# A hybrid conv and latent-attention step with experts: roots from PSUM, summed squares, embeds without a skew, shared last products

## Chip, core and metric

The kernel runs on one NeuronCore of one Trainium2 chip. The metric is the device time of one execution in microseconds (us). An instruction is named below by its line in the kernel, as L1062. VectorE is DVE in the profile, ScalarE is ACT, TensorE is PE (PEld its weight loads), GpSimd is POOL, SyncE is SP; an engine's name with a q behind it is its DMA queue or sequencer.

## What is computed

Two trunk layers run over 264 tokens (256 of a prompt and 8 samples) of width D = 1024. The mixer of layer 0 is a causal convolution module, that of layer 1 a latent attention with a paged cache.

```python
for i in range(DEPTH):
    hn = rmsnorm(h, norm_mix[i])
    mix = conformer_conv(hn, ...) if i % 2 == 0 else mla_mixer(hn, ...)
    h = h + mix
    h = h + hier_moe(rmsnorm(h, norm_ffn[i]), ...)      # 32 experts in 4 groups, the top 2 of one group
    h = h + (p[i] @ ple_w_in[i]) * jax.nn.sigmoid(rmsnorm(h, ple_g[i]) @ ple_w_gate[i])
return rmsnorm(h, norm_final), conv state, ckv, kpe

def rmsnorm(x, g):
    return x * lax.rsqrt(jnp.mean(x * x, axis=-1, keepdims=True) + EPS) * g
```

The third line of the loop body is called the embed below. The attention normalizes its query and key latents with rmsnorm too, and the convolution module has a layernorm.

## The kernel before

Activations lie transposed: `hT` holds h as 8 chunks (KD = 8) of 128 features by 264 tokens. `xnT` holds the chunks times a gain, `sq` their squares. Weights stream from HBM into nine slots of a ring and a few slots beside it, in an order that SyncE's program fixes; a slot is filled again when TensorE has used it. Each engine has its own program, written out in order, and they meet at semaphores. A result of TensorE goes into one of eight PSUM banks, taken in turn: `arrive` waits until a bank is full, `freed` until its reader has let go of it.

**Norms.** ScalarE squares the chunks, TensorE sums them over features with a product by ones, and the sum lands in a bank. VectorE (`inverse_root`, L1062) takes it times 1/n plus EPS into `rstd`, ScalarE (`root`, L1652) takes the square root in place, VectorE (L1064) the reciprocal. The norms are numbered n0 to n6, `lnv`, `q` and `kv`. The products that need a norm mostly run on values without it, and their results are multiplied by `rstd`.

**Squares that VectorE adds.** For n1, n3, n4 and n6 VectorE adds some of the squares into `sq[:, 0]` (`add_square`, L1086), so that TensorE has fewer to sum.

**Router.** While TensorE makes the output products of the mixer chunk by chunk, it also makes the logits (L534). Then `router_tail` forms each token's sum of squares as a column (`token_sums`, L548): once for the chunks that VectorE added, once for chunk 6, once for chunk 7, three products each. ScalarE copies the logits out (L1658, `lgT` lies in `rstd`), takes the root of the columns (L1660), VectorE sums the three parts and scales before it (L1104 to L1106) and inverts after it (L1108). TensorE turns the logits (L563) and the token rows (L646), and L1188 scales the logits; from there VectorE finds group, experts, ranks and slots, with two products of TensorE between (L656, L662), writes the selection matrix `S` (L1281, L1284), and TensorE gathers the tokens (L682).

**Experts.** 17 pairs of experts are worked off in windows (gate and up L703, down L729, combine L744). SyncE's queue loads their weights (L2036); a load whose slot is in use waits until the products of its pair are done.

**Embed.** TensorE makes eight chunks of the gate product. For each, VectorE multiplies it by `rstd` (L1447), ScalarE takes the sigmoid (L1802), VectorE multiplies by `pinT` (L1450) and adds to h (L1452); in layer 0 it also makes the next mixer's gained chunk (L1456). VectorE's loop is skewed: in round m it does L1447 of chunk m, then the rest of chunk m-1, then the square of chunk m-2 into the sum. ScalarE does sigmoid m, then square m-1 (L1805). TensorE's `last_sum` (L524, L526) closes it with two products: the summed squares, then square 7.

**End.** After n6 VectorE makes eight products of h, gain and `rstd` (L1070), and SyncE stores them in two halves (L2092).

## Time and profile before

| | us |
|---|---|
| median of 3 runs | 910.09 |
| lowest and highest | 907.43 and 912.4 |
| profiled execution | 914.86 |
| its span, first to last instruction | 913.2 |
| TensorE busy | 785.9 |
| VectorE busy | 319.0 |
| ScalarE busy | 206.4 |
| GpSimd busy | 58.9 |

The mean granted TensorE clock of the profiled execution is 0.932 of full. Busy shares say little here, since the stages differ: some are bound by TensorE, the expert stages by the weight stream, and in between there are stretches in which the engines hand over to each other. A row of a timeline gives start, duration, engine, line, operation, what is written and read, how many instructions are merged, and in brackets how long the engine was idle before and what ended that. The releaser is inferred; where the one named had long been done, it was another. fp32 products show as two passes each, so one product is x2.

### The profile page before, as it was taken

What the parts mean: (1) busy time and instruction counts of PE and PEld (TensorE: products, weight loads), DVE (VectorE), ACT (ScalarE), POOL (GpSimd) and SP (SyncE); (2) the same over time, 40 slices, a digit from 0 to 9 for tenths busy, and PEclk for the clock granted to TensorE, in tenths of its full rate; (3) what the DMA queues carried; (4) which work ended last, traced back from release to release, by engine and by line L of the source; (5) the groups of instructions that cost most, each with busy time, mean ns of one, the idle gap of its engine ahead of it and who ended that gap; (6) DMA issues with size and microseconds to landing.
All of it is one profiled execution on the core that took longest, in us unless ns stands there. A gap on an engine that the chain in (4) does not pass through costs nothing.

```text
span 913.2 us, 16409 instructions
## 1 busy us (share of the span) xinstructions
PE 785.9 (86%) x6398; PEld 561.3 (61%) x6398; DVE 319.0 (35%) x948; ACT 206.4 (23%) x492; POOL 58.9 (6%) x101
## 2 busy tenths in 40 slices
PE   5999999799889776889899877999998799697894
PEld 5876667666556554558676554678665466364583
DVE  1433333333313212225346464126133133221435
ACT  2100234321111101022226352015321011110322
POOL 2401000000000000000051700000000000000000
PEclk9999999799999989979999988898999899988898
DMA  9853894389999999983166470896699999999601
GB/s 374 324 170 89 275 402 148 146 334 414 417 415 418 414 417 415 412 337 139 47 216 223 127 281 1 354 417 242 231 394 415 418 414 417 416 416 416 243 1 48
DMA packets 59376, 269.35 MB, mean 295 GB/s; under 512 B 7312, under 2 KB 12384, under 8 KB 38176
## 3 DMA queue, kind: packets, MB, share of 16 engines
q1 hardware_dynamic: 53072, 259.22, 71.7%
q10 hardware_dynamic: 3472, 5.13, 1.8%
q0 software_dynamic: 2752, 3.91, 1.5%
q8 instruction: 53, 0.87, 0.4%
q14 instruction: 27, 0.22, 0.1%
HBM read 261.05 MB, written 2.52 MB: 289 GB/s over the span
## 4 chain that ended last, share of the span: by engine, by line
PE 60%; DMA 27%; SPq 5%; DVE 3%; issue 2%; ACT 2%; ACTq 0%; DVEq 0%
PE bank L572 25%; DMA ring<-in_moe_w_up 19%; PE bank L703 10%; PE bank L682 5%; DMA xn_sq<-in_moe_w_up 5%; SPq L2036 4%; PE bank L744 3%; PE bank L729 3%; PE bank L597 2%; PE bank L971 1%; SPq L2028 1%; PE bank L824 1%; PE bank L534 1%; PE bank L829 1%; PE bank L517 1%
## 5 line engine op out<-in xcount | busy, mean ns | idle before, releaser
L703 PE MATMUL bank<-ring,arena 128*32 128x256 f32 x1344 | 116.4, 406 | 21.9 <-DMA arena<-in_moe_w_up 13.5
L572 PE MATMUL bank<-xn_sq,ring 128*128 128x264 f32 x480 | 110.2, 392 | 9.1 <-DMA ring<-in_stream 9.1
L572 PE MATMUL bank<-arena,ring 128*128 128x264 f32 (+1 forms) x456 | 110.3, 397 | 3.0 <-DVE arena L1482 2.2
L572 PEld LDWEIGHTS bank<-xn_sq,ring 128*128 128x128 f32 x480 | 92.5, 193 | 26.0 <-issue 9.9
L682 PEld LDWEIGHTS bank<-arena 128*128 128x128 f32 x864 | 100.5, 196 | 11.3 <-issue 10.4
L682 PE MATMUL bank<-arena 128*128 128x128 f32 (+1 forms) x864 | 103.7, 281 | 4.3 <-DMA ring<-in_moe_w_down 3.8
L1314 DVE TENSOR_TENSOR arena<-arena,bank 128x128 f32<-128x128 f32 x34 | 9.8, 287 | 267.8 <-ACT arena L1735 267.8
L572 PEld LDWEIGHTS bank<-arena,ring 128*128 128x128 f32 x456 | 87.0, 195 | 24.5 <-issue 8.5
L703 PEld LDWEIGHTS bank<-ring,arena 128*32 128x32 f32 x1344 | 65.0, 117 | 60.1 <-issue 41.2
L744 PE MATMUL bank<-arena 128*128 128x264 f32 (+1 forms) x288 | 73.0, 409 | 5.2 <-ACT arena L1751 5.2
L703 PE MATMUL bank<-xn_sq,arena 128*32 128x256 f32 x384 | 56.9, 463 | 17.2 <-DMA ring<-in_moe_w_up 17.2
L744 PEld LDWEIGHTS bank<-arena 128*128 128x128 f32 (+1 forms) x288 | 55.5, 197 | 24.7 <-ACT arena L1751 9.6
L703 PE MATMUL bank<-arena 128*32 128x256 f32 x448 | 61.3, 436 | 10.6 <-DMA xn_sq<-in_moe_w_up 10.6
L1331 DVE TENSOR_TENSOR hT<-hT,bank 128x264 f32<-128x264 f32 x144 | 61.7, 428 | 23.3 <-PE bank L744 21.2
L729 PE MATMUL bank<-ring,arena 128*32 128x512 f32 x336 | 55.7, 619 | 12.6 <-ACT arena L1742 12.6
L1751 ACT COPY arena<-bank 64x512 f32<-64x512 f32 x68 | 39.4, 580 | 72.5 <-PE bank L729 71.7
L703 PEld LDWEIGHTS bank<-xn_sq,arena 128*32 128x32 f32 x384 | 27.5, 133 | 33.4 <-issue 29.4
L703 PEld LDWEIGHTS bank<-arena 128*32 128x32 f32 x448 | 29.7, 125 | 24.8 <-issue 19.8
L1735 ACT ACTIVATE arena<-bank 128x128 f32<-128x128 f32 x34 | 9.4, 277 | 156.2 <-PE bank L703 156.2
L729 PE MATMUL bank<-arena 128*32 128x512 f32 x208 | 38.4, 598 | 6.4 <-ACT arena L1742 6.4
L1954 POOL DMA_DIRECT2D arena<-in_cache_kpeT x64 | 32.0, 501 | 9.0 <-PE bank L971 4.0
L1647 ACT ACTIVATE xn_sq<-hT 128x264 f32<-128x264 f32 x40 | 16.2, 421 | 71.5 <-DVE hT L1078 64.6
(253 smaller groups left out, 835.1 us busy)
## 6 DMA issues: line engine op xcount, KB each, us to landing
ring<-in_moe_w_gate SPq DMA_DIRECT2D x38, 1024.0 KB, 21.7
ring<-in_moe_w_up SPq DMA_DIRECT2D x38, 1024.0 KB, 21.9
ring<-in_moe_w_down SPq DMA_DIRECT2D x38, 1024.0 KB, 22.8
ring<-in_stream SPq DMA_DIRECT2D x35, 1024.0 KB, 9.3
arena<-in_moe_w_down SPq DMA_DIRECT2D x26, 1024.0 KB, 21.0
arena<-in_moe_w_gate SPq DMA_DIRECT2D x14, 1024.0 KB, 19.7
...
```

What stands on the lines that cost most here:

```text
L572: t = mm(ps[:, 0:cols], lhs(k), rhs(k), start=(k == 0), stop=(k == n - 1))
L597: t = mm(ps[CG * b:CG * (b + 1), 0:TP], dg[:, c, TQ * b + q, :], shifted[p % 2][:, b, c % 2, NQ * q:NQ * q + TP], start=(q == 0), stop=(q ...
L682: t = mm(bank[k // 4][:, (k % 4) * n:(k % 4 + 1) * n], XR[:, i, k * P:(k + 1) * P], S[:, j % 2, i, 0:n], start=(i == 0), stop=(i == 2))
L703: t = mm(bank[2 + r][p0:p0 + U, 0:F].rearrange("p (c f) -> p c f", c=2), x, w[i][:, :, k * F + c * P:k * F + (c + 1) * P], start=(k == 0), ...
L729: t = mm(bank[4 + r][p0:p0 + U, :], hidT[:, r, U * (2 * i + c):U * (2 * i + c + 1)], w[i][:, c, h * 512:(h + 1) * 512], start=(c == 0), st ...
L744: mm(bank[CBANK[k % 4]][:, 0:T], O[0:n, j % 2, k * P:(k + 1) * P], gate[0:n, j % 2, :], start=True, stop=True).then_inc(s_cb, 1)
L1314: v.tensor_tensor(hid[:, q % 2, :], sg[:, q % 2, :], bank[2 + q % 2][:, P:2 * P], ALU.mult)\
L1331: v.tensor_tensor(hT[:, k, :], hT[:, k, :], bank[CBANK[k % 4]][:, 0:T], ALU.add).then_inc(s_add, 1)
L1647: s.activation(sq[:, at + k, :], src[:, k, :], ACT.Square).then_inc(s_sq, 1)
L1751: s.copy(O[64 * r:64 * r + 64, j % 2, 512 * h:512 * (h + 1)], bank[4 + r][64 * h:64 * h + 64, :])\
L1954: pool.dma_start(KPT[DR * i:DR * (i + 1), n * PAGE:(n + 1) * PAGE], a["cache_kpeT"][bass.ds(numbers[i][n], 1)].rearrange("o p f -> p (o f)"))\
L2036: sp.dma_start(d, expert_weights(l, number, c)).then_inc(w_in[PLACE[p]], 16)
```

## The change

Six things change.

- Roots. ScalarE's square root reads the sum from PSUM, with scale 1/n and a bias of EPS (a new column of constants), and writes `rstd`; VectorE's scaling is gone. Before the roots of `q` and `kv` ScalarE waits until the banks before are let go, and for `kv` until the query latents are made.
- Router squares. VectorE adds the squares of chunks 1 to 7 for n1 and n4, so `token_sums` is one group of three products. ScalarE takes the roots of the columns from PSUM in two instructions, and takes a root of one element (`early_root`) before it copies the logits.
- Embed. The skew is gone: a chunk is finished in its own round, and the square of chunk m-1 is added between L1447 and the sigmoid's product of chunk m. ScalarE's order stays.
- Last gain. In layer 1's embed VectorE multiplies each finished chunk by the last gain into `pinT`.
- Last products. They are `pinT` times `rstd`: chunks 0 to 4 on VectorE, 5 to 7 on GpSimd.
- Stores. SyncE stores chunks 0 to 2 and 3 to 4, ScalarE's queue stores 5 to 7, from the arena in place of `xnT`.

```diff
@@ -49,7 +49,7 @@
 ARENA = 22936
...
+C_ID, C_ONE, C_TRI, C_ROT, C_EPS, C_COS, C_SIN = 0, 128, 256, 384, 512, 513, 513 + T
 C_MASK = C_SIN + T
...
@@ -150,8 +150,9 @@
 PIN_LAST = [(), (3, 4, 5, 6, 7)]
 
 
-ADDED = {"n1": (0, KD - 3), "n3": (KD - 3, KD - 2), "n4": (2 * KD - 5, KD - 3), "n6": (3 * KD - 8, KD - 2)}
+ADDED = {"n1": (0, KD - 1), "n3": (KD - 1, KD - 2), "n4": (2 * KD - 3, KD - 1), "n6": (3 * KD - 4, KD - 2)}
 LG = 64
+YV = 5
 NORMS = []
...
@@ -536,27 +540,19 @@
                 if k == KD - 1:
                     t.then_inc(is_full(("router", l)), 1)
 
-            def token_sums(l, x):
-
-                key = "n1" if l == 0 else "n4"
-                if x == 0:
-                    open_bank(pe, ("sums", l))
-                    pe.wait_ge(s_acc, sum(ADDED[key]))
-                else:
-                    pe.wait_ge(s_sq, SQ[key] + KD - 2 + x)
+            def token_sums(l):
+
+                ps = open_bank(pe, ("sums", l))
+                pe.wait_ge(s_acc, sum(ADDED["n1" if l == 0 else "n4"]))
                 for i, (t0, n) in enumerate(TILES):
-                    t = mm(bank[taken["sums", l][0]][0:n, 3 * i + x:3 * i + x + 1],
-                           sq[:, KD - 3 + x if x else 0, t0:t0 + n], ones[:, 0:1], start=True, stop=True)
-                if x == 2:
-                    t.then_inc(is_full(("sums", l)), 1)
+                    t = mm(ps[0:n, i:i + 1], sq[:, 0, t0:t0 + n], ones[:, 0:1], start=True, stop=True)
+                t.then_inc(is_full(("sums", l)), 1)
 
             def router_tail(l, norm):
 
                 logits(l, norm, KD - 2)
-                token_sums(l, 0)
-                token_sums(l, 1)
                 logits(l, norm, KD - 1)
-                token_sums(l, 2)
+                token_sums(l)
                 ps = open_bank(pe, ("lg", l))
                 freed(pe, ("router", l))
                 for i, (t0, n) in enumerate(TILES):
@@ -1056,19 +1052,11 @@
                 ins.then_inc(s_dve, 1)
                 dve.wait_ge(s_dve, steps[0])
 
-            def inverse_root(key, n):
-
-                ps = arrive(dve, key)
-                v.tensor_scalar(rstd[:], ps[:, 0:T], 1.0 / n, EPS, ALU.mult, ALU.add).then_inc(is_free(key), 1)
-                dve.wait_ge(s_rs, NORMS.index(key) + 1)
+            def inverse_root(key):
+
+                freed(dve, key)
                 v.reciprocal(rstd[:], rstd[:]).then_inc(s_inv, 1)
                 dve.wait_ge(s_inv, NORMS.index(key) + 1)
-
-            def norm(key, gain, col):
-                inverse_root(key, D)
-                for k in range(KD):
-                    v.scalar_tensor_tensor(out=xnT[:, k, :], in0=hT[:, k, :], scalar=vcol(gain, col + k), in1=rstd[:],
-                                           op0=ALU.mult, op1=ALU.mult).then_inc(s_xn, 1)
 
             def gained(gain, col, k):
                 v.tensor_scalar(xnT[:, k, :], hT[:, k, :], vcol(gain, col + k), None, ALU.mult).then_inc(s_xn, 1)
@@ -1093,18 +1081,14 @@
                     gained(gain, col, k)
                     if 2 <= k < KD - 1:
                         add_square(key, k - 1)
+                    if k >= KD - 2:
+                        add_square(key, k)
 
             def inverse_columns(l):
 
                 key = ("sums", l)
                 at = NORMS.index("n1" if l == 0 else "n4") + 1
-                ps = arrive(dve, key)
-                x = ps[:, 0:9].rearrange("p (i s) -> p i s", i=3)
-                dve.wait_ge(s_zero, 6)
-                v.reduce_sum(rcol[:, 0:2], x[:, 0:2, :], AX.X)
-                step(v.reduce_sum(rcol[0:TS, 2:3], x[0:TS, 2:3, :], AX.X))
-                v.tensor_scalar(rcol[:], rcol[:], 1.0 / D, EPS, ALU.mult, ALU.add).then_inc(is_free(key), 1)
-                dve.wait_ge(s_rs, at)
+                freed(dve, key)
                 v.reciprocal(rcol[:], rcol[:]).then_inc(s_inv, 1)
                 dve.wait_ge(s_inv, at)
 
...
@@ -1440,30 +1424,29 @@
             def embed(l):
 
                 name = "n3" if l == 0 else "n6"
-                for m in range(KD + 1):
-                    if m < KD:
-                        key = ("pg", l, m)
-                        ps = arrive(dve, key)
-                        v.tensor_tensor(sgp[:, m % 2, :], ps[:, 0:T], rstd[:], ALU.mult).then_inc(is_free(key), 1)
-                    if 1 <= m <= KD:
-                        dve.wait_ge(s_gb, KD * l + m)
-                        step(v.tensor_tensor(tgp[:, (m - 1) % 2, :], sgp[:, (m - 1) % 2, :], pinT[:, m - 1, :],
-                                             ALU.mult))
-                        v.tensor_tensor(hT[:, m - 1, :], hT[:, m - 1, :], tgp[:, (m - 1) % 2, :], ALU.add)\
-                         .then_inc(s_ple, 1)
-                        if l == 0:
-                            dve.wait_ge(s_ple, m)
-                            v.tensor_scalar(xaT[:, m - 1, :], hT[:, m - 1, :], vcol("norm_mix", KD + m - 1), None,
-                                            ALU.mult).then_inc(s_xn, 1)
-                    if 3 <= m <= KD:
-                        add_square(name, m - 2)
+                for m in range(KD):
+                    key = ("pg", l, m)
+                    ps = arrive(dve, key)
+                    v.tensor_tensor(sgp[:, m % 2, :], ps[:, 0:T], rstd[:], ALU.mult).then_inc(is_free(key), 1)
+                    if m >= 2:
+                        add_square(name, m - 1)
+                    dve.wait_ge(s_gb, KD * l + m + 1)
+                    step(v.tensor_tensor(tgp[:, m % 2, :], sgp[:, m % 2, :], pinT[:, m, :], ALU.mult))
+                    v.tensor_tensor(hT[:, m, :], hT[:, m, :], tgp[:, m % 2, :], ALU.add).then_inc(s_ple, 1)
+                    dve.wait_ge(s_ple, KD * l + m + 1)
+                    if l == 0:
+                        v.tensor_scalar(xaT[:, m, :], hT[:, m, :], vcol("norm_mix", KD + m), None, ALU.mult)\
+                         .then_inc(s_xn, 1)
+                    else:
+                        v.tensor_scalar(pinT[:, m, :], hT[:, m, :], vcol("norm_final", m), None, ALU.mult)\
+                         .then_inc(s_fin, 1)
                 dve.wait_ge(s_ple, KD * (l + 1))
 
             dve.wait_ge(s_done, 32)
             moe(0)
-            inverse_root("n2", D)
+            inverse_root("n2")
             embed(0)
-            inverse_root("n3", D)
+            inverse_root("n3")
             for m in range(KQ):
                 ps = arrive(dve, ("cq", m))
                 v.tensor_tensor(cqr[:, m, :], ps[:, 0:T], rstd[:], ALU.mult).then_inc(is_free(("cq", m)), 1)
...
@@ -1628,9 +1611,12 @@
             inverse_columns(1)
             dve.wait_ge(s_done, 32 + 64)
             moe(1)
-            inverse_root("n5", D)
+            inverse_root("n5")
             embed(1)
-            norm("n6", "norm_final", 0)
+            inverse_root("n6")
+            dve.wait_ge(s_fin, KD)
+            for k in range(YV):
+                v.tensor_tensor(pinT[:, k, :], pinT[:, k, :], rstd[:], ALU.mult).then_inc(s_yv, 1)
 
         @block.scalar
         def _(act):
@@ -1646,18 +1632,25 @@
                     ready(k)
                     s.activation(sq[:, at + k, :], src[:, k, :], ACT.Square).then_inc(s_sq, 1)
 
-            def root(key):
-
-                freed(act, key)
-                s.activation(rstd[:], rstd[:], ACT.Sqrt).then_inc(s_rs, 1)
+            eps = cst[:, C_EPS:C_EPS + 1]
+
+            def root(key, n=D):
+
+                ps = arrive(act, key)
+                s.activation(rstd[:], ps[:, 0:T], ACT.Sqrt, bias=eps, scale=1.0 / n).then_inc(is_free(key), 1)
 
             def column_root(l):
 
+                s.activation(early_root[:], ones[0:1, 0:1], ACT.Sqrt)
                 key = ("router", l)
                 ps = arrive(act, key)
                 s.copy(lgT, ps[0:G + E, 0:T]).then_inc(is_free(key), 1)
-                freed(act, ("sums", l))
-                s.activation(rcol[:], rcol[:], ACT.Sqrt).then_inc(s_rs, 1)
+                key = ("sums", l)
+                ps = arrive(act, key)
+                act.wait_ge(s_zero, 6)
+                s.activation(rcol[:, 0:2], ps[:, 0:2], ACT.Sqrt, bias=eps, scale=1.0 / D)
+                s.activation(rcol[0:TS, 2:3], ps[0:TS, 2:3], ACT.Sqrt, bias=eps[0:TS], scale=1.0 / D)\
+                 .then_inc(is_free(key), 1)
 
             def h_ready(key):
                 return lambda k: freed(act, key + (k,))
@@ -1810,8 +1803,11 @@
             root("n3")
             squares("q", cqr, KQ, lambda k: freed(act, ("cq", k)))
             squares("kv", kvr, KK, lambda k: freed(act, ("kv", k)), at=KQ)
-            root("q")
-            root("kv")
+            for key in (*(("cq", m) for m in range(KQ)), *(("kv", m) for m in range(KK)), "kpe"):
+                freed(act, key)
+            root("q", QL)
+            act.wait_ge(s_cq, KQ)
+            root("kv", KL)
             for c in range(4):
                 ps = arrive(act, ("qp", c))
                 s.copy(qpr[:, c, :], ps[:, 0:T]).then_inc(is_free(("qp", c)), 1)
@@ -1887,6 +1883,8 @@
             moe(1)
             embed(1)
             root("n6")
+            act.wait_ge(s_yp, KD - YV)
+            act.dma_start(out["y"][:, YV:KD], pinT[:, YV:KD, :]).then_inc(s_y, 16)
 
         def expert_weights(l, e, c):
 
@@ -1975,6 +1973,10 @@
             arrive(pool, ("ss", 0, 1))
             load_kpe(numbers)
             moe(1)
+            pool.wait_ge(s_fin, KD)
+            pool.wait_ge(s_inv, len(NORMS))
+            for k in range(YV, KD):
+                g.tensor_tensor(pinT[:, k, :], pinT[:, k, :], rstd[:], ALU.mult).then_inc(s_yp, 1)
 
         @block.sync
         def _(sp):
@@ -2087,10 +2089,11 @@
             for g in range(G_PG1, NPIECE):
                 fill(g)
 
-            for k in (0, KD // 2):
-                sp.wait_ge(s_xn, 6 * KD + k + KD // 2)
-                sp.dma_start(out["y"][:, k:k + KD // 2], xnT[:, k:k + KD // 2, :]).then_inc(s_y, 16)
-            sp.wait_ge(s_y, 32)
+            for k in (0, YV - 2):
+                n = YV - 2 if k == 0 else 2
+                sp.wait_ge(s_yv, k + n)
+                sp.dma_start(out["y"][:, k:k + n], pinT[:, k:k + n, :]).then_inc(s_y, 16)
+            sp.wait_ge(s_y, 48)
             sp.wait_ge(s_done, 16 * 6)
```

ScalarE's program in layer 0's router, from the squares (L1647) over the logits copy (L1658) to the token rows (L1710), before:

```order
L1647 ACTIVATE xn_sq<-hT 128x264 x8
L1658 COPY rstd<-bank 36x264
L1660 ACT_TABLE_LOAD
L1660 ACTIVATE rcol<-rcol 128x3
L1710 ACTIVATE arena<-bank,rcol 128x64x8 x4
```

and after:

```order
L1633 ACTIVATE xn_sq<-hT 128x264 x8
L1644 ACT_TABLE_LOAD
L1644 ACTIVATE early_root<-cst 1x1
L1647 COPY rstd<-bank 36x264
L1651 ACTIVATE rcol<-bank,cst 128x2
L1652 ACTIVATE rcol<-bank,cst 8x1
L1703 ACTIVATE arena<-bank,rcol 128x64x8 x4
```

The table load has moved ahead of the logits copy, with the root of one element; the column roots read the bank.

VectorE's program at the end of layer 1's embed, from the gate product of chunk 7 (L1447) to the last products, before:

```order
L1447 TENSOR_TENSOR arena<-bank,rstd 128x264
L1450 TENSOR_TENSOR arena<-arena 128x264
L1452 TENSOR_TENSOR hT<-hT,arena 128x264
L1086 TENSOR_TENSOR xn_sq<-xn_sq 128x264
L1450 TENSOR_TENSOR arena<-arena 128x264
L1452 TENSOR_TENSOR hT<-hT,arena 128x264
L1086 TENSOR_TENSOR xn_sq<-xn_sq 128x264
L1062 TENSOR_SCALAR rstd<-bank 128x264
L1064 RECIPROCAL rstd<-rstd 128x264
L1070 SCALAR_TENSOR_TENSOR xn_sq<-hT,vt,rstd 128x264 x8
```

and after (L1430 is the gate product, L1074 the added square, L1441 the last gain):

```order
L1430 TENSOR_TENSOR arena<-bank,rstd 128x264
L1074 TENSOR_TENSOR xn_sq<-xn_sq 128x264
L1434 TENSOR_TENSOR arena<-arena 128x264
L1435 TENSOR_TENSOR hT<-hT,arena 128x264
L1441 TENSOR_SCALAR arena<-hT,vt 128x264
L1058 RECIPROCAL rstd<-rstd 128x264
L1619 TENSOR_TENSOR arena<-arena,rstd 128x264 x5
```

Behind the gate product of chunk 7 stood seven instructions before the reciprocal, now four, and the added square stands ahead of the chunk's own product.

## Rows read from the trace of the kernel before

**Rows 1.** The page's chain that ended last, shares of the span by engine.
```profile
PE 60%; DMA 27%; SPq 5%; DVE 3%; issue 2%; ACT 2%; ACTq 0%; DVEq 0%
```
**Rows 2.** Timeline, layer 0's router: start, us, engine, line, operation, merged instructions [idle before].
```profile
149.15 0.42 ACT L1647 ACTIVATE xn_sq<-hT 128x264 f32<-128x264 f32 x1 [3.90 <-DVE hT L1078]
...
151.14 0.37 ACT L1658 COPY rstd<-bank 36x264 f32<-36x264 f32 x1 [1.57 <-PE bank L534]
...
153.27 0.57 DVE L1188 SCALAR_TENSOR_TENSOR rt_L<-bank,rcol,br 128x36 f32<-128x36 f32 x3
...
158.38 0.94 PE L656 MATMUL bank<-rt_M,cst 128*128 128x32 f32 x6 [0.45 <-DVE rt_M L1217]
...
164.98 8.24 PE L682 MATMUL bank<-arena 128*128 128x128 f32 x48 [3.76 <-DMA ring<-in_moe_w_down]
...
177.82 0.36 SPq L2036 DMA_DIRECT2D ring<-in_moe_w_gate  x1
```
**Rows 3.** Chain of waits, the row transposes of both layers: start, us, what.
```profile
152.48 2.77 PE bank L646 x24
...
618.72 5.31 PE bank L646 x24
```
**Rows 4.** Windows: stretch, length, busy (x) by engine, PEclk, DMA share, GB/s.
```profile
619.00:622.00 3.00, 3.00 (x16) 3.00 (x15) 2.69 (x19) 2.15 (x3) 0.00 (x0) 0.50 0.97 396
```
**Rows 5.** Timeline, the LayerNorm root.
```profile
111.06 0.43 DVE L1062 TENSOR_SCALAR rstd<-bank 128x264 f32<-128x264 f32 x1 [2.03 <-PE bank L517]
111.53 0.42 ACT L1652 ACTIVATE rstd<-rstd 128x264 f32<-128x264 f32 x1 [0.74 <-DVE rstd L1062]
...
115.04 7.67 PE L572 MATMUL bank<-arena,ring 128*128 128x264 f32 x32 [0.46 <-ACT arena L1687]
```
**Rows 6.** One line, a function with a per-partition bias: min/median/max ns, starts, form.
```profile
L1680 ACT ACTIVATE arena<-arena,vt x8: 514/514/514, 27.9 to 87.0; 128x264 f32<-128x264 f32 x8
```
**Rows 7.** Timeline, the end of layer 0's embed.
```profile
436.75 0.43 DVE L1447 TENSOR_TENSOR arena<-bank,rstd 128x264 f32<-128x264 f32 x1 [1.59 <-PE bank L572]
...
437.22 0.42 ACT L1802 ACTIVATE arena<-arena 128x264 f32<-128x264 f32 x1 [2.33 <-DVE arena L1447]
...
439.84 0.42 DVE L1086 TENSOR_TENSOR xn_sq<-xn_sq 128x264 f32<-128x264 f32 x1
...
440.42 1.22 PE L524 MATMUL bank<-xn_sq,cst 128*128 128x264 f32 x2 [3.70 <-DVE xn_sq L1086]
...
442.31 3.92 PE L572 MATMUL bank<-arena,ring 128*128 128x264 f32 x14
```
**Rows 8.** Windows, the sums of layer 0's embed.
```profile
440.00:442.00 2.00, 1.58 (x4) 1.30 (x5) 0.27 (x1) 1.28 (x1) 0.00 (x0) 0.54 0.38 160
```
**Rows 9.** Timeline, TensorE's first product from the query latents.
```profile
469.35 8.25 PE L572 MATMUL bank<-arena,ring 128*128 128x264 f32 x36 [2.20 <-DVE arena L1482]
```
**Rows 10.** Timeline, the end of the kernel.
```profile
902.66 1.28 ACT L1652 ACT_TABLE_LOAD   x1
...
904.93 1.80 DVE L1064 RECIPROCAL rstd<-rstd 128x264 f32<-128x264 f32 x1 [0.49 <-ACT rstd L1652]
906.77 3.32 DVE L1070 SCALAR_TENSOR_TENSOR xn_sq<-hT,vt,rstd 128x264 f32<-128x264 f32 x8
908.50 1.96 SPq L2092 DMA_DIRECT2D out_y<-xn_sq  x2
```
**Rows 11.** DMA issues of the last 14 us: count, KB each, median us to landing.
```profile
out_y<-xn_sq SPq DMA_DIRECT2D x2, 528.0 KB, 2.7
```
**Rows 12.** Two lines whose instructions meet at 29.4: min/median/max ns, starts, form.
```profile
L1138 DVE SCALAR_TENSOR_TENSOR arena<-arena,vt x8: 222/228/1914, 29.4 to 88.0; 128x8 f32<-128x8 f32 x8
...
L1915 POOL TENSOR_TENSOR arena<-arena,cst x8: 1931/1938/2122, 17.7 to 31.2; 128x1024 f32<-128x1024 f32 x8
```
**Rows 13.** Timeline, ScalarE's first table load and what follows it.
```profile
8.62 1.28 ACT L1647 ACT_TABLE_LOAD   x1 [8.62 <-issue]
9.92 2.61 ACT L1647 ACTIVATE xn_sq<-hT 128x264 f32<-128x264 f32 x8
```

14 lines of the change are left out of this document (8 added, 6 removed).

## Prediction

> **What bounds the kernel now.** I read first the page's chain of waits. TensorE makes 60% of it and transfers 27%, VectorE 3%, ScalarE 2% [rows 1]: only work that TensorE waits for, or that stands at the very end, can pay. Then the timelines of the places that the diff touches, to see who waits for whom there.
>
> In layer 0's router TensorE idles twice: 0.45 us before the counts (L656) and 3.76 us before the first gather (L682), both for VectorE's routing steps [rows 2]. (The row names a transfer; the instruction waits for S, which VectorE had just written.) The expert stream starts again only when the first gate and up products are done, at 177.82 [rows 2], and by the page's slices it then fills the DMA engines at about 415 GB/s. They had drained before, so a router that ends earlier moves the whole stage; nothing downstream eats it.
>
> In layer 1's router TensorE doesn't wait: it is the late one. Its row transposes take 5.31 us against 2.77 in layer 0 [rows 3], at a granted clock of 0.50, that is 1.2 GHz [rows 4].
>
> **LayerNorm root.** Today VectorE scales (111.06, 0.43 us), ScalarE takes the root, VectorE inverts, and TensorE waits 0.46 us for the first silu [rows 5]. The diff drops the scaling with its hand-over, 111.06 to 111.53, 0.47 us. But the new root has eps as a per-partition operand; the nearest row with one takes 514 ns [rows 6] against 0.42 for the root without [rows 5]: 0.09 back. Net 0.38, and TensorE was free to use 0.46. I take **0.36**. The roots n0, n2, n5 gain the same, worth nothing: TensorE streams products past them. Bounds for one root: 0.25 to 0.47.
>
> **Router, layer 0.** The last square ends at 149.57 [rows 2]. VectorE adds it (0.42) by 150.05, and three column products instead of nine follow, so the sums stand before ScalarE can use them. ScalarE meanwhile loads the table (1.28) and does the tiny early root: 149.59 + 1.28 + about 0.2 = 151.07, then the copy of the logits, which today starts at 151.14 [rows 2]. So the logits come out only about 0.1 us earlier, after a pause on TensorE of some 0.7 us that it didn't have. The column roots follow the copy, and the inverse is ready near 152.0. L1188, today 153.27 [rows 2], then waits for the logits alone: about 152.4, 0.9 earlier. TensorE's products up to L656 move only 0.1, so of 158.38 one gets the 0.45 of idle and that 0.1: **0.55**. From there VectorE's steps are as before, up to the gather. Bounds 0.3 to 0.9.
>
> **Router, layer 1.** TensorE is late itself there; only its own 0.1 counts: **0.1**, bounds -0.2 to 0.3.
>
> **Embed, layer 0.** Today's skew leaves chunk 7 to a last round: L1447 at 436.75, the sum of squares at 439.84, TensorE starts the sums at 440.42 and the query products at 442.31 [rows 7]. Now chunk 7 is finished in its own round, but one wait is new. ScalarE's order is unchanged: sigmoid of m, then square of m-1. VectorE now adds square m-1 before it takes sigmoid m, so it stands behind both. Counted out for m = 7: L1447 436.75; sigmoid 437.22 (as today); square 6 after it 437.52 to 437.94; add to 438.40; product 438.33 to 438.75, add to h 438.80 to 439.23, square 7 439.27 to 439.69. TensorE does the first sum at 438.56 and the last at 439.83. The query products start at 440.27 (a pair of passes 0.44) or 440.71 (0.88, half clock). Against 442.31 that is 2.04 or 1.60. Today the granted clock is 0.54 in 440 to 442 [rows 8], after 3.70 us of idle; the query products lose about another 0.6 to it (14 passes in 3.92 us against 3.28 at the later spacing). The new idle before work is about 1.6 and 0.9 us. If the clock holds: 2.04 + 0.6 = 2.64. Two to one that it holds: **2.2**, bounds 1.4 to 2.7. Earlier rounds hide it: a round is 2.9 us of VectorE and ScalarE against 3.56 of TensorE's.
>
> **Query root.** TensorE waits 2.20 us for the scaled latents [rows 9]; the root is in front of them. It waits now for VectorE's last eviction too, which is long past. **0.36**, same bounds. The key root gains as much beside 8 us of query products: nothing. That ScalarE waits there for s_cq delays nothing: it did so through VectorE.
>
> **End, root n6.** Square 7 ends today just before 902.66, where the table load begins that ends at 903.94; the inverse starts at 904.93 [rows 10]. Counted as in the embed, square 7 ends at 902.73, 0.09 later; the load ends at 904.02, the sums are there before, the root takes 0.51, the inverse starts at 904.58: **0.35**. Here the load, no longer the scaling, is what ends last.
>
> **End, products and stores.** Today eight fused products take 3.32 us, the first store goes after four (908.50) [rows 10], each takes 2.7 us [rows 11]. Now five plain ones on VectorE (about 0.36 apart, as the centring ones) and three on GpSimd. The trace holds a GpSimd product, 1.94 us for 1024 columns, so 0.5 for 264; and beside it a VectorE instruction of eight columns took 1914 ns instead of 222 [rows 12]. Both engines' products read two SBUF tensors here too. If they take turns: VectorE's third product at +1.95, GpSimd's third at +2.4, VectorE's fifth at +3.05; the last 264 KB store is issued at +3.15 instead of +3.40, a smaller one, and 1.06 MB must pass from +2.7: landing near +5.4 to +5.5 against +6.1. If they run side by side, the third product ends at +1.1 and all has landed near +4.5. I take turns, **0.6**; bounds -0.5 (GpSimd at 0.9 each) to 1.6. By this the trace agrees with the Trainium skill ("SBUF — State Buffer", Who interferes with whom): a VectorE instruction with two SBUF inputs and a GpSimd one that reads SBUF exclude each other for a whole instruction. Without that rule the term would be 1.6.
>
> **Sum.** 0.36 + 0.55 + 0.1 + 2.2 + 0.36 + 0.35 + 0.6 = 4.5 us. The profiled execution took 914.86 (span 913.2), so 910.3 on its scale. It lies 4.8 above the median of the runs, 910.09; nothing says that what it had extra sits in these terms, so the same 4.5 comes off the median: **905.6**. The three runs spread over 5 us, so I call 0.5%, 4.5 us, what a measurement can tell.
>
> **Rivals.**
> *Fuller gain.* The clock holds in the embed (2.64) and the last products run side by side (1.6): 6.0 off, 904.1. For it: a third of these terms is clock luck. Against: the 1914 ns row. 20%.
> *Swallowed.* The expert stream ends when its bytes have passed, whenever the router ends. Then all before it goes (0.36, 0.55, 2.2, 0.36, 0.1), and 0.95 at the end stays: 909.1. Against: the DMA engines are idle when the stream restarts. 13%.
> *Slower: the clock.* The routers get a pause on TensorE that they didn't have. Layer 1's clock fell in just these steps and cost 2.5 us on the transposes [rows 3, 4]; if layer 0's falls there too, and layer 1's gather runs at half clock like layer 0's (8.2 against 5.6 us), 2.5 + 2.6 plus about 0.8 on the products between is 5.9 against the 4.5: 911.5, slower by 1.4. It decides from 4.5 us of added cost at half clock. Against: the first 160 us ran at full clock with pauses in them. 10%.
> *Load in the way.* If a table load holds ScalarE for longer than its own 1.28, the early root pushes the logits back. With 1.4 more per load: +0.8 and +1.2 in the routers and +1.0 at the end instead of -0.55, -0.1 and -0.35: 909.6. Against: a load at 8.62 of 1.28 us is followed by work at 9.92 [rows 13]. 5%. The Trainium skill ("ScalarE: Activation LUTs", What ACT_TABLE_LOAD costs) adds a drain of 1.38 us to every load; the trace doesn't show it.
> The forecast itself: 52%, with its own range 904.0 to 907.2.
>
> **Numbers.** Range 901.5 to 909.5: the terms' bounds sum to 2 to 7, widened by the clock's shifts and the runs' spread; beyond it lies most of the slower rival. Faster by over 0.5% (below 905.5): half of the forecast, nearly all of the fuller gain, 0.48. Slower by over 0.5%: only the slower rival with a bad draw, 0.05. Same: 0.47.
>
> **What would show it.** The roots read from PSUM at 0.5 us, the inverse 0.36 sooner after the sums. In layer 0's router no idle before the counts product, the logits copy still near 151.1. In the embed square 6 right behind sigmoid 7, VectorE idle about 0.5 us before the add, TensorE back 1.6 to 2 us sooner after its last gate product. At the end VectorE's products spread to 3 us by GpSimd's. Wrong would be: query products that start less than 1.4 us sooner; a stream restart that doesn't move; the five products done in 1.9 us.

## The result and the profile after

The changed kernel takes 903.99 us, median of 22 runs (894.95 to 909.28); the kernel before, beside it, 908.9 (22 runs, 905.45 to 914.14). The ratio is 0.9917 with a 95% interval of 0.9895 to 0.9939: faster by 0.6 to 1.1%. Two of the 22 runs count as slow and the ratio leaves them out; the two medians alone would give 0.9946. Run again later it took 903.54 against 910.12, ratio 0.9929 (0.9907 to 0.9951). The forecast was 905.6, so the gain was underrated (4.5 us against 4.9 and 6.6 between the medians of the two series). That the time still lies so near is luck: as the runs show, terms of the forecast were wrong in opposite directions. The profiled execution took 903.49 (span 901.8, mean granted clock 0.939; before 913.2 and 0.932).

The chain of waits of the changed kernel, shares of the span by engine:

```profile
PE 65%; DMA 20%; SPq 5%; ACT 3%; DVE 3%; issue 2%; DVEq 0%; ACTq 0%
```

TensorE's share is 65% instead of 60 [rows 1], the transfers' 20 instead of 27; it is still these two. The places of the prediction, in the timeline of the changed kernel (columns as in [rows 2]): LayerNorm root, router of layer 0, the turn of layer 0's embed, and the end. Rows in between are left out.

```profile
111.03 0.48 ACT L1640 ACTIVATE rstd<-bank,cst 128x264 f32<-128x264 f32 x1 [0.27 <-PE bank L521]
114.60 2.62 PE L568 MATMUL bank<-arena,ring 128*128 128x264 f32 x10
...
150.57 0.35 ACT L1647 COPY rstd<-bank 36x264 f32<-36x264 f32 x1
151.07 0.76 PE L559 MATMUL bank<-cst,rstd 36*128 36x36 f32 x6 [0.60 <-ACT rstd L1647]
151.97 0.57 DVE L1172 SCALAR_TENSOR_TENSOR rt_L<-bank,rcol,br 128x36 f32<-128x36 f32 x3 [0.53 <-PE bank L559]
157.11 0.91 PE L652 MATMUL bank<-rt_M,cst 128*128 128x32 f32 x6
163.77 1.62 PE L678 MATMUL bank<-arena 128*128 128x128 f32 x6 [4.19 <-DVE arena L1268]
...
430.99 0.43 DVE L1430 TENSOR_TENSOR arena<-bank,rstd 128x264 f32<-128x264 f32 x1 [0.69 <-PE bank L568]
432.23 0.43 DVE L1074 TENSOR_TENSOR xn_sq<-xn_sq 128x264 f32<-128x264 f32 x1 [0.80 <-ACT xn_sq L1798]
432.81 0.69 PE L528 MATMUL bank<-xn_sq,cst 128*128 128x264 f32 x2 [1.85 <-DVE xn_sq L1074]
433.98 1.25 PE L530 MATMUL bank<-xn_sq,cst 128*128 128x264 f32 x2 [0.49 <-ACT xn_sq L1798]
435.02 2.41 PE L568 MATMUL bank<-arena,ring 128*128 128x264 f32 x5
...
888.65 1.28 ACT L1640 ACT_TABLE_LOAD   x1
889.94 0.48 ACT L1640 ACTIVATE rstd<-bank,cst 128x264 f32<-128x264 f32 x1
890.52 1.80 DVE L1058 RECIPROCAL rstd<-rstd 128x264 f32<-128x264 f32 x1 [1.96 <-ACT rstd L1640]
892.36 3.44 DVE L1619 TENSOR_TENSOR arena<-arena,rstd 128x264 f32<-128x264 f32 x5
892.48 2.69 POOL L1979 TENSOR_TENSOR arena<-arena,rstd 128x264 f32<-128x264 f32 x3 [281.56 <-DVE rstd L1058]
894.60 1.57 SPq L2095 DMA_DIRECT2D out_y<-arena  x2
895.21 0.35 ACTq L1887 DMA_DIRECT2D out_y<-arena  x1
```

The root from PSUM takes 0.48, as taken; the silu products start 0.44 sooner than the 115.04 of [rows 5], and 0.43 of it is left where the router begins. The counts product comes 1.27 sooner than the 158.38 of [rows 2], 0.84 of it the router's own. In the embed every wait is the one that was counted: VectorE stands 0.80 for square 6 (the prediction's steps give as much, its last paragraph says 0.5), and from the chunk-7 product to the query products it is 4.03 us where it was 5.56 [rows 7]. The five products take 3.44 us and the three on GpSimd 2.69 beside them: they take turns, at a little more than was counted (VectorE through at +3.5 after the reciprocal instead of +3.05, GpSimd at +2.9 instead of +2.4).

What wasn't foreseen is after the stores. The closing instructions of the engines in the changed kernel (duration in ns, start in us):

```profile
L202 DVEq DRAIN  x1: 3474/3474/3474, 892.4 to 892.4; - x1
L202 POOLq DRAIN  x1: 9035/9035/9035, 892.5 to 892.5; - x1
L202 SPq COMPARE_BRANCH  x1: 41/41/41, 898.8 to 898.8; - x1
```

SyncE is through at 898.8, when the stores have landed: 6.5 us after the reciprocal, where it was 6.1 before (906.7 to 912.8) and 5.45 were predicted. But the kernel ends at 901.8, when GpSimd's closing drain does, 6.35 us after GpSimd's last product. Before, that drain ran long ago:

```profile
L200 POOLq DRAIN  x1: 6357/6357/6357, 636.2 to 636.2; - x1
L200 SPq COMPARE_BRANCH  x1: 41/41/41, 912.8 to 912.8; - x1
```

From the end of the reciprocal to the end of the span it is 9.5 us (892.3 to 901.8) where it was 6.5 (906.7 to 913.2). So 3 us are lost at the end, and yet the kernel gained 5 to 7 between the medians: more was won elsewhere than the prediction had. Two differences stand out, both on TensorE. One lies ahead of layer 1's experts and is taken up at the end, under "Router, layer 1". The other is in the chain of the changed kernel, in layer 0's last gate and up group (64 rows) and what follows:

```profile
380.82 3.61 PE bank L699 x59
384.43 1.89 issue
386.32 0.65 PE bank L699 x5
388.33 1.97 PE bank L725 x16
...
391.56 6.05 PE bank L740 x16
```

and of the kernel before:

```profile
383.15 2.79 PE bank L703 x47
385.94 2.85 issue
388.79 2.15 PE bank L703 x17
392.44 3.62 PE bank L729 x16
```

Before, TensorE stops after 47 rows (its products as the profile counts them, a pass each) for 2.85 us, for nothing that the profile shows (in the program the group waits only ahead of its first product), and then runs at half clock (16 down products in 3.62 us instead of 1.97). Now it stops after 59 rows, for 1.89, and the rest of the group and the down products run at full clock. The clock falls all the same, a few us later, in the combine (L740). The windows show it too (PE, PEld, DVE, ACT, POOL busy, granted clock, DMA share, GB/s), before and then after:

```profile
388.00:396.00 8.00, 6.17 (x34) 1.63 (x33) 0.29 (x1) 0.54 (x2) 0.00 (x0) 0.57 0.59 228
```

```profile
386.00:392.00 6.00, 3.32 (x24) 1.10 (x24) 0.29 (x1) 1.71 (x4) 0.00 (x0) 1.00 0.77 300
392.00:400.00 8.00, 8.00 (x22) 5.82 (x21) 5.49 (x16) 4.68 (x9) 0.55 (x1) 0.57 1.00 420
```

Before, the combine has such a fall too (5.58 us for its 16 products), so what is gone is the first of two.

The shift is twelve rows, and twelve are what the change took out of layer 0's sums by token (nine products to three, two passes each).

### The profile page after: what moved, and what is told of

Its sections match the earlier page's. It is cut to its first block, busy times and chain, and to the rows that moved or that the text cites. A ratio compares the mean times of both kernels' runs of the same rounds, so it can differ in the third digit from the quotient of the medians.

```text
span 901.8 us, 16374 instructions
## 1 busy us (share of the span) xinstructions
PE 775.9 (86%) x6374; PEld 553.3 (61%) x6374; DVE 320.6 (36%) x943; ACT 206.0 (23%) x496; POOL 61.6 (7%) x104
## 4 chain that ended last, share of the span: by engine, by line
PE 65%; DMA 20%; SPq 5%; ACT 3%; DVE 3%; issue 2%; DVEq 0%; ACTq 0%
PE bank L568 26%; PE bank L699 11%; DMA ring<-in_moe_w_up 11%; PE bank L678 6%; DMA xn_sq<-in_moe_w_up 5%; PE bank L740 4%; PE bank L725 4%; SPq L2038 3%; PE bank L593 2%; DMA arena<-in_moe_w_up 2%; PE bank L967 1%; SPq L2030 1%; PE bank L521 1%; PE bank L989 1%; PE bank L820 1%
## 5 line engine op out<-in xcount | busy, mean ns | idle before, releaser
L699 PE MATMUL bank<-ring,arena 128*32 128x256 f32 x1344 | 118.7, 408 | 20.3 <-DMA arena<-in_moe_w_up 13.0
L740 PE MATMUL bank<-arena 128*128 128x264 f32 (+1 forms) x288 | 71.1, 401 | 5.2 <-ACT arena L1744 5.2
L740 PEld LDWEIGHTS bank<-arena 128*128 128x128 f32 (+1 forms) x288 | 54.5, 194 | 23.5 <-ACT arena L1744 8.9
L725 PE MATMUL bank<-ring,arena 128*32 128x512 f32 x336 | 53.8, 598 | 12.6 <-ACT arena L1735 12.6
```

The source lines that it names most:

```text
L699: t = mm(bank[2 + r][p0:p0 + U, 0:F].rearrange("p (c f) -> p c f", c=2), x, w[i][:, :, k * F + c * P:k * F + (c + 1) * P], start=(k == 0), ...
L725: t = mm(bank[4 + r][p0:p0 + U, :], hidT[:, r, U * (2 * i + c):U * (2 * i + c + 1)], w[i][:, c, h * 512:(h + 1) * 512], start=(c == 0), st ...
L740: mm(bank[CBANK[k % 4]][:, 0:T], O[0:n, j % 2, k * P:(k + 1) * P], gate[0:n, j % 2, :], start=True, stop=True).then_inc(s_cb, 1)
```

## Experiments

Times are medians, each beside the kernel before in the same series (its medians are 909.8, 909.81, 909.47 and 910.12). Within a kernel, 0.01 more of mean granted clock goes with 6.1 us less (pooled slope over 249 runs), which serves below to compare the means of kernels "at 0.940"; this is a correlation, and part of what it takes out may be the cause itself.

### The end

`e1_all_vector`: the changed kernel, eight products on VectorE.

```diff
-YV = 5
+YV = 8
...
-            act.wait_ge(s_yp, KD - YV)
-            act.dma_start(out["y"][:, YV:KD], pinT[:, YV:KD, :]).then_inc(s_y, 16)
+            act.wait_ge(s_yv, 6)
+            act.dma_start(out["y"][:, 3:6], pinT[:, 3:6, :]).then_inc(s_y, 16)
...
-            for k in range(YV, KD):
-                g.tensor_tensor(pinT[:, k, :], pinT[:, k, :], rstd[:], ALU.mult).then_inc(s_yp, 1)
...
-            for k in (0, YV - 2):
-                n = YV - 2 if k == 0 else 2
+            for k, n in ((0, 3), (6, 2)):
```

> The changed kernel, but all eight last products on VectorE and none on GpSimd; three stores as before (chunks 0 to 2 and 6 to 7 from SyncE's queue, 3 to 5 from ScalarE's). In the changed kernel the stretch from the end of the last reciprocal (892.33) to the end of the span (901.8) is 9.5 us, though the last store has landed at about 898.8. Theory drain: GpSimd's closing drain, which took 9.0 us there from its first product on, some 6.3 us beyond the last one, ends the kernel; with GpSimd done long before, the stretch is eight products at 0.36, a store of 2.7 and about 0.5: 6.0 to 6.3 us, 3.2 to 3.5 less. Rival lock: what costs is that the two engines take turns at SBUF (products over 3.4 us instead of 2.9) and the stores come late; then the stretch shrinks by 0.5 us only, to about 9.

Measured: 899.24 (ratio to before 0.9898, 0.9852 to 0.9945; six runs). Its interval overlaps the changed kernel's, so the proof is in the trace:

```profile
887.02 1.80 DVE L1058 RECIPROCAL rstd<-rstd 128x264 f32<-128x264 f32 x1 [1.99 <-ACT rstd L1640]
888.86 2.84 DVE L1619 TENSOR_TENSOR arena<-arena,rstd 128x264 f32<-128x264 f32 x8
```

```profile
L202 POOLq DRAIN  x1: 6357/6357/6357, 624.4 to 624.4; - x1
L202 SPq COMPARE_BRANCH  x1: 41/41/41, 894.2 to 894.2; - x1
```

The eight products take 2.84 us, less than five did beside GpSimd, and from the end of the reciprocal (888.8) to the end (894.6) it is 5.8 us, 3.7 less than with GpSimd and a little less than was expected. SyncE is through 1.1 us sooner after the reciprocal (5.4 instead of 6.5); the rest of the 3.7 is the drain.

`e2_tiny_pool`: as `e1_all_vector`, and one memset of one element on GpSimd.

```diff
+            pool.wait_ge(s_yv, 5)
+            g.memset(early_root[:], 0.0).then_inc(s_yp, 1)
```

> As e1_all_vector, and GpSimd writes one element once VectorE's fifth product is done: no work to speak of, no SBUF read beside VectorE. Theory drain: its drain starts there, about 1.9 us after the reciprocal, and lasts 6.3 us, so the stretch from the reciprocal's end to the span's end is about 8.3 to 8.5 us, 2.2 more than in e1_all_vector. Rival lock: one element takes no turn; the stretch stays as in e1_all_vector.

Measured: 904.17 (0.9936, 0.9911 to 0.9961), and 8.56 us from the end of the reciprocal (889.94) to the end (898.5). Rows of this kernel:

```profile
891.84 0.09 POOL L1977 MEMSET early_root<- 1x1 f32 x1 [282.35 <-DVE arena L1619]
```

```profile
L202 POOLq DRAIN  x1: 6487/6487/6487, 891.8 to 891.8; - x1
L202 SPq COMPARE_BRANCH  x1: 41/41/41, 895.3 to 895.3; - x1
```

An instruction of 0.09 us costs 2.8 in this stretch: it is not GpSimd's work, but that it works so late.

`e7_only_end`: the kernel before with the end of the change (last gain, five and three products, three stores).

> The kernel before with the end alone: last gain in layer 1's embed, five products on VectorE and three on GpSimd, three stores. Drain theory: GpSimd's last instruction is followed by its closing drain (6.35 us in the changed kernel and in the one with a single-element memset), so from the end of the last reciprocal to the span's end it takes 9.5 us instead of 6.5: 3.0 slower than before at the same clock. The prediction's account: 0.6 faster. In the changed kernel this cost lies under gains elsewhere; here nothing covers it, so the runs should lie 2 to 4 us above before (0.3% slower), and the drain of GpSimd should be the last thing in the trace.

Measured: 916.14 against 909.81, ratio 1.0059 (1.003 to 1.0089). This part alone makes the kernel slower by 3 to 8 us, where 2 to 4 were expected; at 0.940 it is 2.9 (911.8 against 908.9). From the end of the reciprocal (904.5) to the end (914.0) it takes 9.5 us; the drain starts at 904.7 and lasts 9028 ns.

### The parts alone

`e5_only_embed`: the kernel before with the unskewed loop of the embed, and nothing else of the diff.

> The kernel before with the embed's loop of the change alone (a chunk finished in its own round, square m-1 added before the sigmoid's product of chunk m). Over the 71 timed runs so far, within a kernel, 0.01 more of mean granted clock goes with 6.3 us less (slopes of -386 to -723 us per unit). Theory A, own steps alone: from the last L1447 product to the query products 5.56 us in the kernel before and 4.03 in the changed one, so 1.5 less here at layer 0, and 0.1 more at layer 1's (square 7 is counted 0.1 later); mean clock as before, 0.936; time 1.4 below before. Theory B, the embed also carries the clock's gain: TensorE idles 2.34 us there instead of 3.70, and the mean clock goes to 0.941 as in the changed kernel, which is 3 us more; time 4.4 below before. In both the last product to the query products is 4.0 to 4.1 us in the trace.

Measured: 907.72, ratio 0.9966 (0.9938 to 0.9994). From the chunk-7 product (436.52) to the query products (440.55) it is 4.03 us. At 0.940 it lies 1.8 below the kernel before (907.1 against 908.9): theory A, the own steps.

`e8_only_roots`: the kernel before with the roots of `root` from PSUM, `inverse_columns` as before.

> The kernel before with the roots from PSUM alone (all norms but the two routers' columns). Terms: LayerNorm root 0.43 as read in the changed kernel, query root 0.34, n6 root by which the table load ends last: the kernel before lost 0.99 us from the load's start at 902.66 to ... the inverse at 904.93 (2.27), the changed one 1.87 (888.65 to 890.52), so 0.40. Sum 1.2 below before at the same clock of 0.936. A rival, by which the extra 3 to 4 us of the changed kernel come from here (sooner normalized products everywhere, n0, n2, n5 included): 4 us below before. In the trace the silu products of the LayerNorm start 0.43 sooner and the scaled latents' wait is 0.34 shorter (2.20 to 1.86).

Measured: 908.77, ratio 0.9988 (0.9962 to 1.0014): about the own 1.2, and not the extra; by itself no measurable change. The wait for the scaled latents is 1.87 instead of 2.20 [rows 9].

`e6_only_router`: the kernel before with `ADDED`, `token_sums`, `router_tail`, `inverse_columns` and `column_root` of the change.

> The kernel before with the router's part alone (squares 1 to 7 added by VectorE, three column products, roots of the columns from PSUM, the early root). Own steps: in the changed kernel the counts product of layer 0 came 0.84 us sooner than the LayerNorm root explains, so 0.8 less up to the first gather, as little or less in layer 1: 0.8 to 1.4 below before at the same clock of 0.936. Theory B' (the router carries the clock's gain, since VectorE's idle-free steps bring the gather sooner): clock 0.941 or more, 4 us below before. Theory C (the pause on TensorE before the transposes costs clock, as the kernel without the early root, at 0.950 against 0.941, suggests): clock no higher than before's, or lower, and the time 0 to 1 below before. In the trace: logits copy near 151.0, counts product 0.84 sooner than in the kernel before (158.38 to 157.5).

Measured: 904.57, ratio 0.9914 (0.9881 to 0.9948), at a clock of 0.939, in six runs. This part alone gains 5 to 11 us, as much as the whole change does. Of the three theories none fits: the own steps are too small, and the clock is hardly higher (0.939 against 0.937).

`b2_before_again`: the kernel before, profiled once more.

> The kernel before once more, for a second profile. In its first profile (914.86, above its median of 909 to 910) the expert stage of layer 1 took 230.4 us from the first down products to the embed's long run, against 224.4 in the changed kernel, and 224.7 to 225.5 in the three kernels that hold only one part of the change and the old router or the new. If the first profile was a slow draw there: 225 to 226 now, and 233 to 234 in layer 0. If the stage is longer in this kernel: 230 again.

Stage 0 and stage 1 stand for the expert stages of the two layers, from the end of the first gate and up group to the embed's long run of gate products. Measured: stage 1 took 225.6 us (645.67 to 871.24), stage 0 233.1 (176.85 to 409.92). The 230.4 us of stage 1 in the first profile of before were a draw, so 5 of the 11.4 us between the first two profiles mean nothing. Stage 0 is another matter: it takes 232.9 to 234.2 us in the five profiles with the old sums by token, and 230.2 to 232.0 in eight of the ten profiles with the new ones, the two others being `e4_no_early_root` (226.9) and `e9_filled_pause` (233.2).

### The pause and the clock

`e4_no_early_root`: the changed kernel without its early root.

```diff
-                s.activation(early_root[:], ones[0:1, 0:1], ACT.Sqrt)
```

> The changed kernel without the root of one element ahead of the logits copy in both routers, so that the table load falls behind the copy. My account of the router: TensorE's 0.60 us wait before turning the logits (L559) goes, so its products start 0.7 us sooner; the column roots come behind the load, the inverse at about 152.15 instead of 151.26, so the scaled logits are 0.3 us later. Layer 1's router, in which TensorE is late, gets 0.7 us shorter from the last mixer product to the counts product; layer 0's gets within 0.2 us of what it was. Rival: the early root is worth its place, and both routers get longer by 0.3 or more.

Measured: 898.45 (0.9881, 0.9842 to 0.992; six runs), at a clock of 0.950: 5.5 us less than the changed kernel, where a few tenths were expected, though the two intervals overlap. TensorE has no pause of 0.60 us ahead of L559 then, and in layer 0 the scaled logits come 0.2 later after square 7 (3.41 instead of 3.24), as expected. The profile shows where most of it was won: the combine of stage 0 doesn't fall to half clock,

```profile
391.27 3.83 PE bank L740 x16
```

against 6.05 us for the same products in the changed kernel (and 5.8 to 6.2 in the other seven profiles with a stop after 59 rows). That is not this kernel's alone to have: the changed kernel has runs of 894.95 and 895.56 at 0.952.

`e9_filled_pause`: the changed kernel, its three column products made twice.

```diff
-                for i, (t0, n) in enumerate(TILES):
+                for i, (t0, n) in 2 * list(enumerate(TILES)):
```

> The changed kernel with the router's three column products made twice, in the same place: 0.70 us more of TensorE's work, which fills its pause of 0.60 us ahead of the turning of the logits and moves nothing else by more than 0.1 (the column roots by some 0.2 to 0.4, which the logits' scaling hides in part). Pause theory: the early root costs time because TensorE pauses, and the granted clock falls in what follows; filled, the mean clock rises from 0.941 towards 0.950 and the time falls by 3 to 5, to 899 to 901. Rival (the early root costs only because it pushes the logits back by 0.6): clock 0.941, time as the changed kernel or 0.2 above, 904.

Measured: 907.41 (0.9946, 0.9914 to 0.9978), clock 0.938. The pause theory falls: the pause is filled (L559 follows without one), and the clock isn't higher. Instead the median is 3.4 above that of the changed kernel (not clear of the runs' spread: the intervals overlap), and the chain shows a place.

```profile
379.86 3.21 PE bank L699 x53
383.07 2.27 issue
```

Its last gate and up group stops after 53 rows, six fewer than in the changed kernel, and six rows are what was added to layer 0's sums. Stage 0 takes 233.2 us.

`f1_pad6`: the changed kernel, with twelve rows more where TensorE idles 4.19 us in layer 0.

```diff
+                if l == 0:
+                    for _ in range(6):
+                        mm(bank[7][0:1, 0:1], ones[:, 0:1], ones[:, 0:1], start=True, stop=True)
```

> The changed kernel with six one-column products more on TensorE in layer 0, ahead of the first gather, where TensorE idles 4.19 us: twelve rows, as many as the change took out of the router's sums, and no time on a path. Code theory: near the end of layer 0's expert stage TensorE stops in the middle of a gate-and-up group (64 rows) for nothing that the profile shows. With the router's old sums it stops after 47 rows for 2.46 to 2.85 us and its clock is halved in what follows; with the change after 59 rows for 1.80 to 1.90 us at full clock; with three products added, after 53 rows for 2.27 us and at half clock. So the stop sits at a fixed place of the instruction stream. Here: after 47 rows, 2.4 to 2.9 us, down products of 3.2 to 3.7 us instead of 1.97, the stage 233 to 234 us instead of 230.4, and 2.5 to 3.5 us more than the changed kernel. Rival (the stop belongs to the weight loads, and its place is set by when the stream restarts): after 59 rows for 1.9 us, 230.4, and the time of the changed kernel.

Measured: 907.16, against 903.54 of the changed kernel on the same chip (below): 3.6 slower, for six products that delay nothing (the two intervals, 0.9949 to 0.9998 and 0.9907 to 0.9951, just touch). The chain of this kernel:

```profile
385.12 2.79 PE bank L702 x47
387.91 2.73 issue
390.64 2.22 PE bank L702 x17
394.36 3.55 PE bank L728 x16
```

The picture of the kernel before, as the stream's fixed place has it; the rival, 59 rows and 1.9 us, is refuted. Stage 0 takes 233.9 us.

The size needs care. The profiled execution lost more, ahead of the added products, which run at 166.07: the row transposes took 5.31 us, at a granted clock of 0.68 in 150 to 155, and the stage began at 179.78. In `a2_after_again`, the same program up to there, it is

```profile
152.25 2.77 PE bank L642 x24
175.84 2.79 PE bank L755 x24
```

Of the 3.9 us, 3.4 stand already at the counts product (161.13 against 157.69), ahead of the added ones: a fall of the clock that they can't have caused. The same fall stands in three other profiles (`e2_tiny_pool`, `f2_router_pad6`, and `e5_only_embed`, which has the old sums and no pause). How often it came in the timed runs isn't known. The length of the stage is free of it: 232.9 to 234.2 us, mean 233.6, in the seven profiles with a stop after 47 rows, and 226.9 to 232.0, mean 230.3, in the nine with one after 59. By this the place of the stop is worth 3.3 us.

`f2_router_pad6`: the router's part alone, with the same six products.

> The kernel with the router's part of the change alone, with the same six one-column products: TensorE's instruction stream is as long again as before at the end of layer 0's expert stage. The kernel without them lay 5 to 8 us below before where its own steps give 1 to 2. Code theory: stop after 47 rows for 2.4 to 2.9 us, stage 233 to 234 us (231.8 without them), and only 3 to 5 us below before. Rival (the rest of the router's gain has nothing to do with the stop): as without them, 904 to 905, stage 231 to 232.

Measured: 907.54 (0.9964, 0.994 to 0.9988), 3.0 above `e6_only_router`; stop after 47 rows for 2.76 us, stage 0 233.9 us. So some 3 of the 5 us that the router's part gained are the place of the stop, with the same reserve: the two were timed in different series, their intervals overlap, and this profile too has 1.7 us of slower row transposes ahead of the stage.

`a2_after_again`: the changed kernel.

> The changed kernel again, on the same chip as the two with products added. Stop after 59 rows for 1.8 to 1.9 us, stage 0 of 230.4 us, median 902 to 905, mean granted clock near 0.941; from the end of the last reciprocal to the span's end 9.5 us.

Measured: 903.54, stop after 59 rows for 1.90, from reciprocal to end 9.4. One miss: stage 0 took 232.0 us, not 230.4, since more of what follows the last combine ran at half clock.

What ends the stop can be read in the rows of the DMA queues. A block of instructions (q8, 0.02 MB) and a smaller one (q14) pass in the windows named here, and TensorE goes on about 1.3 us after the start of the second (times to a quarter of a us):

| kernel | rows before the stop | stop | q8 block | q14 block | TensorE goes on |
|---|---|---|---|---|---|
| before | 47 | 385.94, 2.85 us | 386.0 | 387.5 | 388.79 |
| f1 | 47 | 387.91, 2.73 | 387.75 | 389.25 | 390.64 |
| f2 | 47 | 385.39, 2.76 | 385.5 | 386.75 | 388.14 |
| e9 | 53 | 383.07, 2.27 | 382.75 | 384.0 | 385.34 |
| after | 59 | 384.43, 1.89 | 383.5 | 385.0 | 386.32 |

In rows of the DMA queues, of the kernel before (window 386.0 to 386.25) and the changed one (383.5 to 383.75):

```profile
q8 instruction: 1, 0.02, 25.7%
```

```profile
q8 instruction: 1, 0.02, 25.8%
```

That TensorE runs out of instructions there is an inference from these times and from the place counted in rows, which moved by 6 and 12 exactly as rows were added. Why this block comes late isn't shown: the page of the profile counts 53 blocks on q8, and no other pause of this kind over 1 us stands in the chains of waits. The Trainium skill ("Runtime: NRT & Kernel Launch", Instruction fetch mechanics) says that instructions come in 16 KiB blocks and that their fetch is mostly hidden. The size of the blocks agrees here (53 blocks are 0.87 MB on the page of the profile); if the stop is a fetch, this one is not hidden, by 1.8 to 2.9 us.

### Versions that go further

`e3_square_first`: the changed kernel, ScalarE's square m-1 ahead of sigmoid m.

> The changed kernel, but in both embeds ScalarE takes the square of chunk m-1 before the sigmoid of chunk m. Theory new wait: VectorE's idle time of 0.80 us before each added square is the wait that the change brought in, because the square stands behind the sigmoid. With the square first the add runs right behind the gate product, the last gate product to the start of the last sum falls from 3.0 us (430.99 to 433.98, and 885.69 to 888.68) to about 2.35, twice; 1.3 us less in all. Rival: the sigmoid's own wait for VectorE is what counts and nothing moves.

Measured: 903.05 (0.9911, 0.9876 to 0.9947). VectorE's wait of 0.80 for the square is gone and the last sum comes 2.33 us after the chunk-7 product instead of 2.99, as expected; in the time (seven runs) it is too small to see.

`c1_load_after_copy`: eight products on VectorE, no early root in the routers, square first, and in the embeds a one-element root between the last sigmoid and square 7.

> All the findings in one kernel: the changed kernel without the early root in the routers (the table load falls behind the copy of the logits again), all eight last products on VectorE and nothing on GpSimd at the end, square m-1 ahead of sigmoid m, and the root's table loaded early in the embeds, by a one-element root between the last sigmoid and square 7. Against the changed kernel: without the early root 5.5 less (898.45 against 903.99), the drain 3 to 3.7 less, square first 0.65 at layer 0 and 0.65 at layer 1, the early load in the embeds 0.5 at the end and nothing at layer 0. If these add: about 10 less, 893 to 895. Rival: the 5.5 was the clock's luck in few runs (6) and the terms on TensorE's idle time are swallowed by a lower granted clock: 898 to 899.

Measured: 899.89 (0.9863, 0.983 to 0.9895; six runs), clock 0.942. The rival was right but for 0.9 us: without the early root the clock was not 0.950 here, and stage 0's combine took 6.03 us again. Of the 5.5 us of `e4_no_early_root` at least the greater part was the clock in its six runs; why it held there stays open.

`c2_load_before_square`: the same with the routers' early root between squares 6 and 7.

```diff
+                    if name in ("n1", "n4") and k == n - 1:
+                        s.activation(early_root[:], ones[0:1, 0:1], ACT.Sqrt)
```

> As the kernel c1, but with the router's table load kept early and off every path: the one-element root stands between square 6 and square 7, where ScalarE idles 3.90 us in the changed kernel, instead of behind square 7. TensorE then has no pause of 0.60 us ahead of the turning of the logits (it is there in the changed kernel, not in the one without the early root), and the column roots come right behind the sums: scaled logits (151.97 in the changed kernel, 152.19 without the early root) near 151.4. If it is TensorE's pause that costs the clock: mean clock 0.949 or more as without the early root (0.950, against 0.941 with it), and 0.2 to 0.8 less than c1. If it is that VectorE's steps come later relative to TensorE's: the clock is as in the changed kernel, 0.941, and the time 4 to 5 above c1.

Measured: 898.9 (0.9871, 0.9843 to 0.9898; eight runs), clock 0.942. Load and pause are gone; from square 7 (147.74) to the scaled logits (150.33) it is 2.59 us instead of 3.24 (148.73 to 151.97 in the changed kernel). It is not told apart from c1, and both lie 4 to 5 us below the changed kernel and some 10 below the kernel before.

## Why the prediction was off

Step by step, in its own terms (us gained):

| term | predicted | measured |
|---|---|---|
| LayerNorm root | 0.36 | 0.43 |
| router, layer 0 | 0.55 | 0.84 in its steps, and 3.0 to 3.6 by the stop (3.3 by the length of stage 0) |
| router, layer 1 | 0.1 | 2.0 on average, clock included |
| embed, layer 0 | 2.2 | 1.5 |
| query root | 0.36 | 0.33 |
| root n6 | 0.35 | 0.40 |
| end, products and stores | 0.6 | -3.0 |

*Right.* The roots, and the embed counted instruction by instruction; of its two clock cases the lower one came, 1.60 counted and 1.53 measured, since TensorE still fell to 0.61 of the full clock in 435 to 438. That products of VectorE and GpSimd take turns. That the table load ends last ahead of root n6 (2.27 us from load to reciprocal in [rows 10], 1.87 now). That TensorE pauses ahead of L559 (0.60 us, 0.7 counted).

*The step that failed first: "end, products and stores".* It ended the kernel with the landing of the stores. The landing itself came at +6.5 instead of +5.45, near the worse of its bounds (0.4 lost, where -0.5 was the bound): turns cost a sixth more than counted, and the last store was issued at +3.5. Behind it the last to finish was GpSimd's closing drain, 2.6 us later. The trace of before held its length, 6357 ns at 636.2, but there it lay under other work, and the prediction has no term for it. Sum of the own steps with it: 0.43 + 0.84 + 1.5 + 0.33 + 0.40 - 3.0 = 0.5. By these steps the change should have been worth almost nothing.

*The step that failed second: "router, layer 0".* "So a router that ends earlier moves the whole stage; nothing downstream eats it" is true for the restart (1.97 sooner, 177.82 to 175.85; 1.21 of it stand at the start of the gather, the rest is the gather at a faster clock, 7.47 us instead of 8.23, which the kernel before also had in its second profile, 6.93), but the stage itself isn't a constant. Twelve fewer rows on TensorE moved a stop near its end, and the half clock right behind the longer stop went: 3.0 (f2 against e6) and 3.6 us (f1 against the changed kernel), 3.3 by the stage. That the row count moves the stop is shown; that the stop is a fetch of instructions is argued. With this the own steps come to 3.5 to 4.1, and with layer 1's router to 5.5 to 6.1, against 4.9 and 6.6 us between the medians of the two series.

*Router, layer 1, also mis-sized.* From the last output product to the stage's start it was 32.0 to 33.7 us in five profiles with the old sums (33.67, 32.82, 32.83, 33.66, 32.00) and 30.3 to 31.9 in the eight with the new sums and the early root (31.77, 30.26, 30.26, 31.77, 30.26, 30.26, 31.77, 31.87). So TensorE's own 0.1 wasn't all, and "TensorE is late itself" no longer holds: in the changed kernel it waits there for ScalarE's copy of the logits. In two of the old ones ScalarE's table load behind the copy stands in the chain, and where it doesn't, the row transposes ran at 4.2 to 5.3 us. The prediction had taken one profile's half clock there for the state of things. In the first two profiles, from the end of the last output product to the turning of the logits it is 2.83 us instead of 3.12 (611.20 less 608.37, 617.61 less 614.49), and from there to the counts 7.76 instead of 9.39, the same products at a faster clock: 0.3 is order and 1.6 clock. For the mean of 2.0 it wasn't separated.

The rivals: *swallowed by the stream* is refuted by the restart and the embeds that follow it; *slower by the clock* too, for the kernel as a whole (0.941 against 0.936), though the fall in layer 0's transposes that it names does come: in 3 of the 12 profiles with the new sums, and in 1 of the 5 with the old. *Fuller gain* came near the time, 904.1, but by another way; products side by side didn't happen. *A load in the way* by more than its 1.28 us didn't happen: the root starts at 889.94, as the load ends.
